# Matmuls on constant tiles in TensorE's waits around three norm and router stages of a two-block model

## What is computed

```python
# first block
h = concat(meta_tokens, x)                      # 16 + 256 rows
mix = hybrid_mixer(rms_norm(h, g0), ...)        # latent attention beside a gated convolution, then w_out
h = h + rms_norm(mix, g_post_mix)
t = rms_norm(h, g_pre_ffn)                      # stage n1
h = h + rms_norm(shared(t) + experts(t, router(t)), g_post_ffn)
# second block
xn = rmsnorm(h, attn_norm_g)                    # stage n2
h = h + concat(diff_attention(xn), retention(xn)) @ w_out
xn = rmsnorm(h, ffn_norm_g)                     # stage n3
h = h + experts_2(xn, router_2(xn))
out = rmsnorm(h, final_norm_g)
```

## Time and profile before

| | |
|---|---|
| time, median of 3 runs | 1110.01 us (1107.6 to 1110.35) |
| span of the profiled execution | 1109.3 us |
| mean granted TensorE clock | 0.977 |
| TensorE busy | 1021.5 us, 92% |
| VectorE / ScalarE / GpSimd busy | 338.6 / 155.8 / 35.7 us |
| HBM read | 338.56 MB, 306 GB/s over the span |

### The profile page before, as it was taken

The page is one execution under the profiler, slowest core; times in us unless marked ns, Lnnn a source line. Parts: engine busy times, 40 slices in busy tenths (PEclk is TensorE's granted clock), DMA queues, the critical chain, the costliest instruction groups (busy, mean ns, idle before and its releaser), DMA issues.

```text
span 1109.3 us, 12940 instructions
## 1 busy us (share of the span) xinstructions
PE 1021.5 (92%) x4993; PEld 594.4 (54%) x4993; DVE 338.6 (31%) x691; ACT 155.8 (14%) x357; POOL 35.7 (3%) x67
## 2 busy tenths in 40 slices
PE   6998969999999999979999599999998989898985
PEld 4676537676766676566654535353535344343532
DVE  2344144334334334330420522222131222221213
ACT  3232132000001000121341200000000000000002
POOL 3000220000000000000001100000000000000000
PEclk9999988999999999989999799999999999999998
DMA  9930332588998888944333189999999999999994
GB/s 322 343 120 1 121 126 77 194 357 365 415 373 364 365 361 366 392 175 169 120 134 109 47 347 421 420 422 422 421 422 422 422 422 421 422 423 421 422 421 179
DMA packets 61124, 340.13 MB, mean 307 GB/s; under 512 B 10300, under 2 KB 11344, under 8 KB 23840
## 3 DMA queue, kind: packets, MB, share of 16 engines
q1 hardware_dynamic: 55536, 337.60, 75.7%
q10 hardware_dynamic: 5136, 1.87, 0.7%
q0 software_dynamic: 416, 0.16, 0.1%
HBM read 338.56 MB, written 1.05 MB: 306 GB/s over the span
## 4 chain that ended last, share of the span: by engine, by line
PE 78%; DMA 13%; DVE 5%; ACT 2%; issue 1%; SPq 0%; DVEq 0%; ACTq 0%
PE ps L707 25%; DMA ring<-in_expert_w_up_dram 13%; PE ps L739 12%; PE ps L693 11%; PE ps L1543 7%; PE ps L1685 4%; PE ps L755 4%; PE ps L1756 4%; PE ps L1720 1%; PE ps L1533 1%; PE ps L1658 1%; PE ps L719 1%; PE ps L1626 1%; ACT xs L964 1%; PE ps L925 1%
## 5 line engine op out<-in xcount | busy, mean ns | idle before, releaser
L707 PE MATMUL ps<-ring,work 128*64 128x256 f32 (+1 forms) x2048 | 341.7, 489 | 26.0 <-DMA ring<-in_expert_w_up_dram 16.2
L707 PEld LDWEIGHTS ps<-ring,work 128*64 128x64 f32 x2048 | 149.2, 138 | 219.7 <-issue 173.6
L739 PE MATMUL ps<-ring,work 128*64 128x512 f32 x768 | 172.1, 596 | 0.8 <-ACT work L532 0.7
L693 PEld LDWEIGHTS ps<-parts 128*128 128x128 f32 x512 | 125.7, 336 | 11.1 <-issue 10.4
L693 PE MATMUL ps<-parts 128*128 128x256 f32 x512 | 128.7, 407 | 1.6 <-DVE parts L577 1.6
L739 PEld LDWEIGHTS ps<-ring,work 128*64 128x64 f32 x768 | 52.4, 137 | 97.8 <-issue 96.6
L606 DVE TENSOR_TENSOR work<-work,ps 128x256 f32<-128x256 f32 (+1 forms) x32 | 17.8, 555 | 269.6 <-PE ps L707 269.6
L1543 PE MATMUL ps<-xT,ring 128*128 128x256 f32 (+1 forms) x384 | 88.6, 389 | 1.3 <-issue 1.3
L1543 PEld LDWEIGHTS ps<-xT,ring 128*128 128x128 f32 x384 | 73.6, 194 | 14.3 <-issue 2.2
L755 PE MATMUL ps<-parts 128*128 128x512 f32 x256 | 74.3, 412 | 1.6 <-DVE parts L627 1.6
L597 DVE TENSOR_TENSOR work<-ps,gk 128x512 f32<-128x512 f32 x64 | 44.3, 692 | 96.2 <-PE ps L693 96.2
(11 more groups left out here) (301 smaller groups left out, 613.0 us busy)
## 6 DMA issues: line engine op xcount, KB each, us to landing
ring<-in_expert_w_gate_dram SPq DMA_DIRECT2D x64, 1024.0 KB, 19.2
ring<-in_expert_w_up_dram SPq DMA_DIRECT2D x64, 1024.0 KB, 22.6
ring<-in_expert_w_down_dram SPq DMA_DIRECT2D x64, 1024.0 KB, 16.8
ring<-in_w_gate_dram SPq DMA_DIRECT2D x32, 1024.0 KB, 8.1
ring<-in_w_up_dram SPq DMA_DIRECT2D x32, 1024.0 KB, 9.8
ring<-in_w_down_dram SPq DMA_DIRECT2D x32, 1024.0 KB, 6.8
ring<-in_w_in_dram SPq DMA_DIRECT2D x18, 1024.0 KB, 13.5
ring<-in_w_out_dram SPq DMA_DIRECT2D x8, 1024.0 KB, 10.9
```

The source lines that it names most:

```text
L693: mm = pe.matmul(ps[:, 6 + b, c * 2 * P:(c + 1) * 2 * P], v[:, tt, feature::KC].bitcast(F32R), onehot[:, tt, :].bitcast(F32R), start=(k + ...
L707: mm = pe.matmul(ps[CAP * e:CAP * e + CAP, 4 + which, 0:ff], xgT[:, k0 + k, P * odd + CAP * e:P * odd + CAP * e + CAP], chunks[e][:, k, :] ...
L739: mm = pe.matmul(ps[CAP * e:CAP * e + CAP, 6 + half, :], hT[:, c0 + k, CAP * e:CAP * e + CAP], chunks[e][:, k, 512 * half:512 * half + 512 ...
```

## The change

A helper `idle_matmuls(pe, bank, count)` is new. It issues `count` matmuls on TensorE with `before` as weights and `ones` as the moving tile into the first 128 columns of one PSUM bank, with no wait and no semaphore update. Nothing reads the result. It is called in six places: in n1 ahead of each tile's `turn_tokens` (6, then 16, into bank 5), in n2 ahead of the wait for both tiles' `h` (30, into bank 4), in n3 ahead of each tile's `turn_tokens` (5 and 5, into bank 0), and between `turn_logits` and `positions_of` of n3 (18, into bank 5). In each place it stands ahead of the wait on TensorE's queue.

```diff
+        def idle_matmuls(pe, bank, count):
+
+            for _ in range(count):
+                pe.matmul(ps[:, bank, 0:P], before[:, :], ones[:, :], start=True, stop=True, skip_group_check=True)
+
...
             pe.wait_ge(ev("mixc"), 4)
             for tt in range(TT):
+                idle_matmuls(pe, 5, (6, 16)[tt])
                 turn_tokens(pe, "n1", tt)
                 turned(pe, "n1", tt)
                 logits(pe, "m1", tt)
...
             moe_tensor(pe, moes[0])
+            idle_matmuls(pe, 4, 30)
             pe.wait_ge(*nth("h_two", 2))
             for tt in range(TT):
                 turn_tokens(pe, "n2", tt)
...
             project(base2 + 12, mixT, lambda tt, half: 1 + 2 * tt + half, ev("out2p"), 8, turn_heads)
             for tt in range(TT):
+                idle_matmuls(pe, 0, (5, 5)[tt])
                 turn_tokens(pe, "n3", tt)
                 turned(pe, "n3", tt)
                 logits(pe, "m2", tt)
             turn_logits(pe, "m2")
+            idle_matmuls(pe, 5, 18)
             positions_of(pe, "m2")
             moe_tensor(pe, moes[1])
```

## The result

| | before | after |
|---|---|---|
| time, median of 10 runs each | 1109.99 us (1107.6 to 1111.51) | 1113.65 us (1112.14 to 1115.09) |
| ratio, 95% interval | | 1.0038 [1.0028, 1.0047] |
| span of the profiled execution | 1109.3 us | 1112.1 us |
| mean granted clock | 0.977 | 0.985 |

The account below looks back on a forecast made before the run. Untouched expert stretches start only when the stage ahead ends, so changes in the three norm and router stages count whole. Span 1109.3 - 1.0 - 1.7 + 0.4 = 1107.0, plus 0.7 to the median: 1107.7 us; range 1103.6 to 1111.0.

Parts of the forecast that it names:

- What bounds the kernel: Both expert stretches start when the stage ahead ends, so a microsecond in any norm and router stage arrives whole.
- Price of an added matmul: Each matmul is two records of 0.112 us, 0.224 us in all at 2.4 GHz, twice that at 1.2 GHz.
- Stage one: n1, 6 and 16 matmuls: hidden in waits, clock's fall delayed, not avoided; 1.0 us won, bounds 0.4 and 4.2.
- unchanged rise: n1: if the clock still rises at 174.2, the projection starts 0.83 us earlier at half speed; net 0.4 us won.
- the ceiling: n1: clock at 2.4 GHz throughout speeds transposes (0.83 us), logits (1.66) and projection (1.7); together 4.2 us won.
- Stage two: n2, thirty matmuls: 6.7 us in an 8.08 us wait; 1.7 us won, between 0.8 lost and 3.3 won.
- Stage three: n3: five and five lose 1.5 us, eighteen win 1.1 in L940 to L944; 0.4 us lost.
- Gather: n3, gather L693: wins nothing from the higher clock, 7.96 us at 1.2 GHz and 8.14 at 2.4 GHz.
- From span to median: Whole kernel: the profiled span lies 0.7 us under the median of 1110.0, so 0.7 is added to 1107.0.
- (a): Rival: clock stays at 2.4 GHz through n1, 4.2 us won instead of 1.0; 1104.5 us, chance 0.32.
- (b): Rival: slower, lower clock falls on n3's first gate matmuls after the gather, 1.7 us; 1111.9 us, chance 0.13.
- (c): Rival: matmuls don't count as activity or aren't run as written; 1111.5 us at most, 1110.0 if they vanish, chance 0.05.

Follow-up runs that it names:

- n1_24: Against the kernel before: only n1's matmuls added, six and twenty-four instead of six and sixteen; 1105.92 us, ratio [0.9957, 0.9981].
- n2_only: The change with only n2's thirty matmuls kept, all other groups left out; 1113.4 us, ratio to before [1.0027, 1.0052].
- n3_55: The change with only n3's five and five kept, all other groups left out; 1113.76 us, and 1112.21 us when run again.
- n3_only: The change with only n3's groups kept (5, 5 and 18), n1's and n2's left out; 1111.93 us, ratio to before [1.0013, 1.0034].
- no_n2: The change without n2's thirty matmuls, all other groups kept; 1111.93 us, ratio to before [1.0011, 1.0033].

## Why the prediction was wrong, step by step

- **What bounds the kernel**: right. A difference in a stage's length arrives at the end; m1 is 265.12 us in both traces. But a changed stage can also move the lower clock in parts that are not changed (4.3 us in the stage showed as 3.3 in `n1_24`).
- **Price of an added matmul**: right. Sixteen in n1 took 3.84 us (3.6 said), eighteen in n3 4.29 (4.0); a group of ten records shows 1.28 and moves what follows by 1.1 us.
- **Stage one**: right mechanism, smaller size. The forecast took 1.0 us out of 0.4 to 4.2, and 0.4 came, by the working that it gave for an unchanged rise: the transposes' gain less the projection's longer time at half speed. The row nearest to the case was the lower end itself. Twenty-four reach the ceiling (`n1_24`); they change the number and the rest that is left at once, so whether it is the rest that decides was not tested.
- **Stage two**: this step failed. It said of the branch that "below 1.4 us it is covered", and took the covered case; the stretch from the last scatter to the projection was to lose 1.7 us and grew by 5.8. By the rows of after: the first matmul comes 473.10 - 467.19 = 5.9 us after the last scatter; sixty records at 0.112 would be 6.7 us, together 12.6 against a wait of 8.08, so 4.5 lost. They took 9.4 us up to the transposes, since the clock had fallen in the break: 2.7 more. The transposes and the wait behind them then took 3.2 instead of 4.7 us: 1.45 won. 4.5 + 2.7 - 1.45 = 5.8. The gain that I had reasoned out was real, and it stood behind a delay five times as large. I had named the branch as a cost without a row, and gave it no bound: the wait that hides it could have hidden anything up to 8.08 us. The honest upper end of the cost was 8.1 + 6.7 - 8.1 = 6.7 us lost, not 0.8. Alone the thirty cost 4.4 us (`n2_only`) where 1.7 won was forecast. Beside the other groups the medians show no cost of theirs that is clear of noise (3.7 and 3.0 with them, 3.0 without), since the lower clock then falls on the projection and the first gates in their place.
- **Stage three**: +1.5 as forecast (`n3_55`), the first five worth 0.5 and the second 1.0. The eighteen bring L940 to L944 to 0.91 us (1.2 said) but win 0.6, not 1.1, since VectorE's wait before the gather takes 0.4 back. Net +0.9 instead of +0.4. Gather: indifferent, as said. A loss outside the stage was not foreseen: `n3_only` took 2.9 us more (1.4 to 3.8), of which the stage has 0.9 and the break in n2 0.4; the rest is open.
- **From span to median**: wrong by a microsecond. Each execution's time lies 1.7 to 1.9 us over its span, which the three times and the one span of before did not show. So the profiled execution took about 1111.0 us, 1.0 above its median, and "its span lies 0.7 under the median" compared two different things. Had I subtracted my 2.3 us from the median, the same number would have come out; as a difference, -2.3 was forecast and +3.7 measured.
- **Rivals**: (a), the clock staying up in n1, needed 24 matmuls. (b), the fall on the gate matmuls, did not occur in after, but did in `no_n2`. (c) fell with the first trace. None of them was the mechanism behind the largest loss: an engine that has nothing to wait for and yet no instructions. The chance of 0.05 for slower rested on (b)'s price alone.

## What to carry to other kernels

A wait on an engine may hide something that isn't in the row: here 8.08 us "for VectorE" also covered up to 6.3 us in which TensorE had no instructions to run. Before filling a wait, look at what stands between it and the work ahead; behind a branch or a loop's end, count the room as unknown until a trace with work in it shows it. Fill a wait whole or leave it: in stage n1 sixteen matmuls won 0.4 us and twenty-four 4.3, of which the time showed 3.3; and put no filler where there is no idle time before the next instruction (0.5 and 1.0 us lost for five and five).

## What was unexpected of the hardware

- The same branch took 0.5 to 0.6 us in some programs and 5.6 to 6.3 us in others, which differ only in matmuls elsewhere. With a short branch a break of 3.97 us could come fourteen records later (`n2_only`). Each of these breaks ended 2.5 to 2.6 us after a packet of an instruction queue started.
- Added matmuls behind a place change it: four of the five kernels that differ from before only in n3 (five traces) had their last two transposes of n2 0.2 to 0.7 us apart from the rest, 130 to 140 us ahead of the first added matmul. The two start 2.4 to 2.6 us after a packet of q8 starts, so this is a wait for instructions too. It fits a layout of the instructions in memory that moved, which was not tested.
- The lower clock wandered in untouched parts: the second attention took 126.05 us in some executions and 127.6 to 128.2 in others, m1 263.4 or 265.1, by whether one stretch of it lay on TensorE's path. Such steps of 1.7 us are as large as most terms of the forecast, so one profiled execution does not price them. They can also cancel: the five traces with the short m1 and without the thirty all have the long attention, so that a gain in one place is gone in the next.
